# Moving a small tile in SBUF: the activation pair stands 192 instead of 64 bytes (modulo 256) behind the weight ring

## What is computed

```python
for l in range(DEPTH):
    a = hybrid_mixer(rms_norm(x, pre_mix_g[l]), ...)
    x = x + rms_norm(a, post_mix_g[l])
    c = memory_cross_attention(rms_norm(x, pre_xattn_g[l]), rms_norm(mem, mem_g[l]), ...)
    x = x + rms_norm(c, post_xattn_g[l])
    hdn = jnp.square(jax.nn.relu(rms_norm(x, pre_mlp_g[l]) @ w_up[l]))
    x = x + rms_norm(hdn @ w_down[l], post_mlp_g[l])
```

## Time and profile before

| | |
|---|---|
| median of three executions | 1424.11 us |
| profiled execution, whole | 1419.34 us |
| its span, first to last instruction | 1417.5 us |
| TensorE matmuls | 10479 |
| granted TensorE clock, mean over the span | 0.980 |

### The profile page before, as it was taken

One profiled execution on the slowest core, in us unless ns is written; L12 is line 12 of the kernel. 1 busy time (PEld: TensorE's weight loads), 2 busy tenths in 40 slices (PEclk: granted clock), 3 DMA queues, 4 the chain that ended last, 5 costly groups with the idle time before them and its releaser, 6 DMA issues.

```text
span 1417.5 us, 23851 instructions
## 1 busy us (share of the span) xinstructions
PE 1335.4 (94%) x10479; PEld 1284.0 (91%) x10479; DVE 826.5 (58%) x874; ACT 661.6 (47%) x934; POOL 88.2 (6%) x65
## 2 busy tenths in 40 slices
PE   4998989999999999898999999999989998899998
PEld 3987988989999999798898999998888897899998
DVE  5467436566653475743665665447848766666542
ACT  4354435455544444543544554434455544455432
POOL 3000002020000000000201000001100100000000
PEclk8999999999999999999999999999989999999999
DMA  6724234334655543414434365655343132356553
GB/s 192 228 74 149 88 122 149 119 119 141 205 191 190 186 120 93 146 54 157 149 94 145 120 209 183 204 182 152 115 139 120 40 110 89 100 173 204 179 198 100
DMA packets 195574, 202.94 MB, mean 143 GB/s; under 512 B 5716, under 2 KB 191847, under 8 KB 195471
## 3 DMA queue, kind: packets, MB, share of 16 engines
q1 hardware_dynamic: 192704, 194.82, 42.9%
q0 software_dynamic: 2464, 5.99, 1.4%
q10 hardware_dynamic: 303, 0.61, 0.1%
HBM read 200.33 MB, written 3.16 MB: 144 GB/s over the span
## 4 chain that ended last, share of the span: by engine, by line
PE 75%; DVE 11%; ACT 8%; issue 3%; DMA 2%; POOL 0%; ACTq 0%; DVEq 0%; POOLq 0%
PE bank L561 13%; PE bank L562 13%; PE bank L563 13%; PE bank L2085 6%; PE bank L2083 6%; PE bank L2087 6%; DVE w_lo L525 4%; ACT w_hi L515 3%; PE bank L602 2%; PE bank L604 2%; PE bank L603 2%; DVE head_sq L1547 1%; PE bank L1945 1%; PE bank L1976 1%; PE bank L1923 1%
## 5 line engine op out<-in xcount | busy, mean ns | idle before, releaser
L525 DVE TENSOR_TENSOR w_lo<-raw,w_hi 128x2048 fp32r<-128x2048 f32 (+7 forms) x210 | 424.1, 2030 | 426.4 <-ACT w_hi L515 426.1
L515 ACT ACTIVATE w_hi<-raw 128x2048 fp32r<-128x2048 f32 (+7 forms) x210 | 354.8, 1704 | 447.5 <-PE bank L563 169.9
L561 PE MATMUL bank<-act_hi,w_hi 128*128 128x256 f32 x1096 | 308.6, 282 | 0.0
L562 PE MATMUL bank<-act_lo,w_hi 128*128 128x256 f32 x1096 | 306.8, 280 | 0.0
L563 PE MATMUL bank<-act_hi,w_lo 128*128 128x256 f32 x1096 | 305.9, 279 | 0.0
L2083 PE MATMUL bank<-h_hi,w_hi 128*128 128x256 f32 x768 | 212.2, 276 | 0.0
L2085 PE MATMUL bank<-h_lo,w_hi 128*128 128x256 f32 x768 | 212.0, 276 | 0.0
L2087 PE MATMUL bank<-h_hi,w_lo 128*128 128x256 f32 x768 | 212.0, 276 | 0.0
L561 PEld LDWEIGHTS bank<-act_hi,w_hi 128*128 128x128 f32 x1096 | 206.1, 188 | 0.6 <-DVE act_lo L1764 0.3
L562 PEld LDWEIGHTS bank<-act_lo,w_hi 128*128 128x128 f32 x1096 | 205.8, 188 | 0.3
L563 PEld LDWEIGHTS bank<-act_hi,w_lo 128*128 128x128 f32 x1096 | 205.0, 187 | 0.0
(11 more groups left out here) (333 smaller groups left out, 2249.7 us busy)
## 6 DMA issues: line engine op xcount, KB each, us to landing
raw<-in_w_up_dram SPq DMA_DIRECT2D x32, 1024.0 KB, 5.5
raw<-in_w_down_dram SPq DMA_DIRECT2D x32, 1024.0 KB, 5.0
raw<-in_w_ff_dram SPq DMA_DIRECT2D x32, 1024.0 KB, 5.3
raw<-in_w_in_dram SPq DMA_DIRECT2D x23, 1024.0 KB, 5.4
raw<-in_w_xk_dram SPq DMA_DIRECT2D x8, 1024.0 KB, 5.6
raw<-in_w_xv_dram SPq DMA_DIRECT2D x8, 1024.0 KB, 5.0
raw<-in_w_mix_out_dram SPq DMA_DIRECT2D x8, 1024.0 KB, 5.0
raw<-in_w_xq_dram SPq DMA_DIRECT2D x8, 1024.0 KB, 4.9
```

Source lines behind the costliest of these rows:

```text
L515: ins = act.activation(d, r, ACT.Copy)
L525: ins = dve.tensor_tensor(d, r, h.bitcast(F32), ALU.subtract)
L561: pe.matmul(o, stat_hi, mov_hi, start=first, stop=False)
L562: pe.matmul(o, stat_hi, mov_lo, start=False, stop=False)
```

## The change

`small` (64 bytes) is taken from between `x_t` and `act_hi` and stands behind `row_inv`; `neg_max` (192 bytes) takes its place in front of `act_hi`. No instruction, wait, size or order changes.

```diff
         x_t = sb("x_t", [P, KD, T])
-        small = sb("small", [P, 16])
+        neg_max = sb("neg_max", [P, 48])
         act_hi = sb("act_hi", [P, KD, T], F32R)
         act_lo = sb("act_lo", [P, KD, T], F32R)
...
         rstd_c = sb("rstd_c", [P, 2, T])
-        neg_max = sb("neg_max", [P, 48])
         row_sum = sb("row_sum", [P, 48])
         row_inv = sb("row_inv", [P, 48])
+        small = sb("small", [P, 16])
         qk_dil = sb("qk_dil", [P, KD, T])
```

## The result

The changed kernel took 1429.18 us (median of 20 runs, 1426.01 to 1438.39); the kernel before, run beside it, 1424.21 us (20 runs, 1418.30 to 1428.25). The ratio is **1.0044**, with a 95% interval of 1.0028 to 1.0059: slower by 0.44%, just inside the 0.5% that the prediction called no change. Forecast were 1431 us and 0.47%. The profiled execution took 1431.11 us (span 1429.3), 11.8 us more than the profiled one of before. That one was among the quickest of its kernel, this one lies a little above its median, so by the medians 6.8 of the 11.8 us belong to the choice of executions and 5.0 to the change.

What follows compares the result with a forecast made beforehand. TensorE's matmul rate bounds the kernel (busy 1335.4 of 1417.5 us). Down halves +8.5, other column slabs -2.5, row slabs +0.7, other tiles 0 gave +6.7 us: median 1431, own range 1426 to 1436, 8 in 10 range 1410 to 1436.

Steps and rivals of the forecast that it cites:

- The place counts, modulo 256 bytes: All matmul streams: distance between moving and stationary operand modulo 256 matters; 113.3 ns fast against 117.8 ns slow.
- Rival C: Whole kernel: place has no effect of its own, up halves stay at 117.8 ns, time 1424 us; chance 0.09.
- The up halves enter slow again at 192: Feed-forward up halves, 2016 matmuls, distance 64 to 192: slow again with 281 ns records, gain 0; all fast, 9.0 us.
- rival A: Feed-forward up halves enter fast and stay fast, gaining 9.0 us, down halves unchanged: 1412 us (1407 to 1416); chance 0.28.
- The down halves lose 8.5 us because the rhythm carries over: Feed-forward down halves: no distance change at the boundary any more, slow rhythm continues from the up halves, +8.5 us.
- The other column slabs, -2.5 us: Activation pair moving outside the up halves, 2112 matmuls: some 780 become fast, taken as -2.5 us; bounds 0 and -9.0.
- Row slabs, +0.7 us: Slabs with weights moving, 864 matmuls, distance 192 to 64: some 160 lose 4.45 ns, +0.7 us; bounds 0 and +0.8.
- Any third rate would be wrong altogether.: Sign against the forecast: any rate besides the fast and slow ones, for instance slower transposes or a new weight wait.

Runs made afterwards that it cites:

- experiments 1 and 2: 1: changed kernel with only the activation pair moved, other tiles back (modulo 256), 1.0037. 2: kernel before with the pair at 320, everything behind moved 256 bytes, 1.0001.
- experiments 7 to 12: Kernel before with only the activation pair moved, to distances 0, 32, 96, 128, 160, 224: ratios 1.0052, 0.9991, 1.0039, 1.0046, 1.0033, 1.0096.
- Experiment 3: Changed kernel plus four 128-column float32 transposes between last up slab and first down slab of each feed-forward part: ratio 1.0006 to the kernel before.
- experiment 5: Kernel before (pair at 64) plus four float32 transposes ahead of the first up slab of each feed-forward part: 1433.66 us, ratio 1.0049.
- experiments 4 and 6: Changed kernel plus, 4: four float32 transposes ahead of each up half, 0.9947; 6: three distance-0 matmuls ahead of up halves and slabs 28, 2, 13, 0.9946.

## Why the prediction was right, point by point

- **The place counts, modulo 256 bytes.** Right, on experiments 1 and 2 and, for the distance against the place of one tile, on the row slabs of experiments 7 to 12. The Trainium skill ("SBUF — State Buffer", section "Who interferes with whom": PE reads through two ports of its own and never waits on anyone) would, as the prediction read it, have given 0 for every row of the table above; the rates from 116.7 to 120.0 ns, at a granted clock of 1.00, disagree with that reading. No run here shows TensorE waiting for another engine's reads. Rival C falls, too: the marks changed and the down halves slowed.
- **The up halves enter slow again at 192.** The result was right, three of three in the changed kernel, with the mark changed to 281 ns. The reason given was too strong. It said that a start straight behind float32 matmuls, with a first record of 0.47 us, is slow each time. Half slab 28 of the first block, the very example of the earlier trace rows, was fast in the changed kernel, and so were the pairs at 36 us and later that begin in the same way:

```profile
279.29 0.47 PE L616 MATMUL bank<-o_hi,w_hi 128*128 128x256 f32 x1
279.60 0.28 PE L617 MATMUL bank<-o_lo,w_hi 128*128 128x256 f32 x1
...
L616 PE MATMUL bank<-o_hi,w_hi 128*128 128x256 f32 x19 | 5.2, 276 | 0.0
...
L602 PE MATMUL bank<-act_hi,w_hi 128*128 128x256 f32 x27 | 7.5, 276 | 0.0
```

(The timeline at 279 us and the groups at 285 to 297 and 37 to 46 us, changed kernel.) Of the up entries themselves, nine in the changed kernel and experiments 1 and 3, seven were slow and two fast. In all fourteen traces together such starts at 192 were fast 31 times of 87 (at the other distances never, of 127). Four cases of four were too few to call it a rule; the same step of 0.31 us led into both rhythms, and rival A could not have been ruled out from the trace of before. That all three entries of the changed kernel fell slow was in part luck, and the forecast needed it.
- **The down halves lose 8.5 us because the rhythm carries over.** Right in place and size: 3.4, 3.4 and 1.7 us, the last eight down slabs fast. Experiment 3 takes it back with a break at the boundary and nothing else. The half of the step that said *why* they were fast before, that a change of distance throws the stream out, holds in part only: 64 to 192 did not do it in two blocks of experiment 5, nor 224 to 192 in three blocks. And the kernel before shows that no change of distance is needed: slow row slabs at 192 run without a pause into the attention outputs, also at 192, and these are fast (rows of the kernel before at 202 to 206 and 208 to 212 us):

```profile
L561 PE MATMUL bank<-w_hi,act_hi 128*128 128x256 f32 x13 | 3.7, 281 | 0.0
...
L561 PE MATMUL bank<-o_hi,w_hi 128*128 128x256 f32 x13 | 3.6, 276 | 0.0
```

So it is, six times of six, in the three kernels with the pair at 64. What changes there is which tile moves. The prediction read distance alone as the thing that throws the stream out, and this row was in its trace.
- **The other column slabs, -2.5 us.** Right in size, for the pair: matmuls with the pair moving that run fast rose from 92 to 579, 487 x 4.45 = 2.2 us. Some 780 were forecast in the count and cut to -2.5 us for caution. The attention outputs, which did not move and were priced at 0, went from 604 fast to 817, worth another 0.9 us; as their state depends on the slabs before them, they should have had bounds.
- **Row slabs, +0.7 us.** Right: 169 matmuls at 113.3 ns before, 21 after, 148 x 4.45 = 0.7 us. The marks follow the distance here as well: at distance 64 the record is 280 ns. At 192 the attention output of the third block, 281 before, happened to be fast (rows of the changed kernel at 638.5 to 642 and 1164 to 1178 us):

```profile
L561 PE MATMUL bank<-w_hi,act_hi 128*128 128x256 f32 x11 | 3.1, 280 | 0.0
...
L561 PE MATMUL bank<-o_hi,w_hi 128*128 128x256 f32 x42 | 11.6, 276 | 0.0
```

- **The sum.** +8.5 - 2.5 + 0.7 = +6.7 forecast; with the counts of the trace in place of the estimates, 8.5 - 2.2 + 0.7 - 0.9 = +6.1; measured +5.0 by medians, 6.3 by the ratio (4.0 to 8.4 with its interval). The profiled 11.8 are these 6 and clock and spread, as shown above. The time lay 2 us from the forecast.
- **"Any third rate would be wrong altogether."** There was none in this change, but the table has five more (116.7, 117.3, 118.3, 118.7, 120.0). The picture of one fast and one slow level was an accident of looking at 64 and 192.

What stays open: what in the chip keeps the rhythm, why the same entry falls into one or the other, whether a break at the entry works by what it executes or by the time it takes, and how the phase among three matmuls decides at a boundary. No run here takes these apart. Every count of entries comes from one profiled execution per kernel, and the blocks of one kernel mostly fall alike, so the counts stand on fewer independent cases than they name.

## What to carry to other kernels

Where a kernel is bound by a long back-to-back stream of matmuls, compare the time from start to start over a few hundred of them between stretches of equal shape; if they differ by a few per cent at full clock, the place of the moving tile against the stationary one (modulo 256 bytes) and the way in which the stream began are suspects, and a padding tile changes the one, a few short matmuls ahead of it the other. Price both together: a slow rhythm can run on into the next tile's stretch, so what a padding costs may show up where nothing moved. And try a cheap break (0.36 to 0.54 us) only in front of the long streams, together with the place, and measure it: at 192 it was worth 1.0% between two otherwise equal kernels, at 64 it cost 0.5%, and ahead of other streams at 192 such breaks mostly did nothing. Look, too, whether the faster stream reaches a slab before its weights are written.

## What the runs showed of the hardware

- Float32r matmuls of 256 columns with a 128x128 stationary operand follow each other at 113.3 ns at best, at a granted clock of 1.00, or at a slow rate that depends on the distance of the moving from the stationary operand modulo 256 bytes: 120.0, 116.7, 117.8, 120.0, 118.7, 117.3, 117.8 and 118.3 ns in the up halves for 0 to 224 in steps of 32. It is the same when the two operands change roles (96, 224, 32 and 160). At 32, 128 and 160 a second or third slow rate was seen in other stretches. The fast rate was seen at 64 and 192 only.
- At 192 both rates exist, and each keeps itself over 1440 matmuls (from the up entry to the end of the down half, slow in the changed kernel, fast in experiments 4 and 6), through changes of tile, bank and slab. A pause of 0.16 us, a wait for weights, was enough to go from fast to slow, twice.
- Four float32 transposes of 128 columns ahead of a stream at 192 led to the fast rate at three up entries, three boundaries and 26 of 28 output turnings (14 kernels, two each), 32 of 34. Eight such transposes ahead of other streams at 192 (slab 13, slab 19, slab 29) led to it in 5 of 42. Three matmuls at distance 0: all three up entries and three of six other stretches. Float32 matmuls of 256 columns: two up entries of nine, 31 streams of 87 in all. Four transposes ahead of a stream at 64: none of three.
- The slow rhythm has a period of three matmuls in the records (one at 280 among two at 279 for distance 64, one load in three at 192 ns for distance 192), and which of the three it is can differ between blocks of one execution.
